# Branches B and C of a fused two-block kernel: two pieces of attention work in one step of TensorE, and the last tile summed from PSUM by VectorE

## The chip, the cores and the metric

One core of one Trainium2 chip runs the whole program. The metric is the device time of one execution in microseconds (us); lower is better. A measurement of one execution repeats within a few tenths of a per mille here (3111.25 to 3112.31 in three runs).

## The reference

Two blocks run one after the other on a sequence of 256 tokens of width 2048, in fp32. The first is one layer: a gated linear recurrence, and dilated attention in three groups of eight heads. The second, which the change touches, is a layer that is applied twice with other weights. Its core, shortened:

```python
def _hybrid_layer(x, ...):
    h = _rmsnorm(x, g_pre)
    ... = jnp.split(h @ w_in, SPLIT_POINTS, axis=-1)      # 2048 x 16192 weights
    o_a = latent attention, 8 heads of 128 (+ 64 rotated)
    # branch B: 8 heads, two softmax maps of width 64 each, values of 128
    a = softmax(q1 @ k1.T * s + mask) - lam * softmax(q2 @ k2.T * s + mask)
    o_b = _rmsnorm(a @ v, b_g_sub) * (1.0 - lam_init)
    # branch C: 8 heads of 128, one map, a bias by distance
    o_c = softmax(q @ k.T * s + bias) @ v
    y = sum over the three branches n of
        sigmoid(gate_n) * ((o_n * silu(z_n)) @ w_branch[n])
    return y @ w_out

for l in range(2):
    x = x + _hybrid_layer(x, l, ...)
```

With 256 tokens the attention is small: per head two score maps of 128 queries by 256 and 128 keys. Nearly all work is in the products with the weights, and every weight is used once.

## The kernel before

All activations are kept feature-major in SBUF (tiles of 128 features by 256 tokens). A weight product runs in **units**: a unit is 1024 rows by 256 columns of one weight matrix (1 MB), in two **halves** of 512 rows. SyncE loads a half into `raw` (line 383). ScalarE copies it into the high part of `hl` in a rounded 32-bit format (`hi`, line 952), and VectorE writes what that leaves out into the low part (`lo`, line 1310). TensorE then does, for each 128 rows and 128 columns, a wide matmul (high weights by high and low activations, 512 columns) and a narrow one (low weights by high activations, 256 columns); both are in `mm`, line 537. So a unit is 32 matmuls and a half 16. `hl` and `raw` hold two units: the split of unit n + 2 begins when TensorE has finished with the same half of unit n. Two units make a chunk of 256 output columns, whose two parts in PSUM (`pg`) are put together in SBUF: ScalarE copies the correction (`copy_corr`, line 960) and VectorE adds it (`join`, line 1317).

Attention is done by pairs of heads, four pairs per branch and layer, so branches B and C have eight pairs each in all. A pair has twelve units (0 to 11): queries, keys, values, a gate `z`, and four units of the branch's big gate. The small steps of the pair's attention stand between units, in PSUM `pa`, in full fp32. The order is written out by hand in the tables `EVENTS` (for TensorE), `ACT_EVENTS` (ScalarE, which for branch C is the same table) and `DVE_EVENTS` (VectorE). A word is a step with the numbers it runs over:

- `u9` is unit 9, `h20` half 20, that is the first half of unit 10 (`h21` its second, `h22` and `h23` those of unit 11)
- `s0`, `s1`: the scores of head 0 and 1 (TensorE, line 781); maxima (VectorE, lines 1584 and 1588) and exponentials (ScalarE, line 1133)
- `x0`, `x1`: VectorE turns the exponentials into probabilities (lines 1597 to 1605; line 1605 is the last operation of a head of branch B, and raises `probs_ready`)
- `t0`, `t1`: TensorE transposes the probabilities (line 788), after a wait for `probs_ready` and, for `t1` in branch B, for `pt_ready`; ScalarE copies the result to SBUF (line 1193) and raises `pt_ready`
- `p0`, `p1`: TensorE multiplies the values by them (lines 798 and 799); then, in branch C, VectorE's product with the gate (line 1719) and the split of the result by ScalarE (line 1139) and VectorE (`lo0`, `lo1`, line 1724); in branch B ScalarE's square (line 1196)
- `n0-1`: in branch B the norm of the result (line 889)

The engines run their tables side by side and meet at semaphores. Inside one engine the order of the table is the order of the instructions. A place at which TensorE's stream of line 537 is interrupted by such small steps is called a **break** below. The table `SIDE` names, by unit, the 128-row steps for which the wide matmuls of both columns come first and then both narrow ones: `FIRST` is the first step of a half or of the unit that begins there, `FIFTH` the fifth, where the second half begins.

The table's order around the change, before:

```python
"B": events("u0-4 norm u5-6 s0 u7-8 t0 s1 u9 p0 h20 t1 h21 p1 h22 n0-1 h23"),
"C": events("u0-4 norm u5-6 s0-1 u7-8 t0-1 u9 p0 u10 p1 u11"),
```

The last product of the program (`w_out` of layer two, added to `xres`) ends by bank: TensorE finishes the first 128 columns of the last chunk, raises `bank_done`, and then does the second (`last_unit_by_bank`, line 659). For each, ScalarE copies the correction (lines 967 and 969), VectorE joins it with the main part into `corr` (line 1325) and adds the sum to `xres` (lines 1875 and 1877), and SyncE stores it (lines 528 and 530).

Of the kernel before, what the change touches and what calls it, by code (L numbers as in the profile page):

```python
# [18 lines left out]
ALU = mybir.AluOpType  # L19
# [4 lines left out]
S = 256  # L24
D = 2048
NT = D // P
UC = 2048
CH = 256
NCH = D // CH
# [31 lines left out]
def events(text):  # L61

    out = []
    for word in text.split():
        what = word.rstrip("0123456789-")
        first, _, last = word[len(what):].partition("-")
        out += [(what, j) for j in range(int(first or 0), int(last or first or 0) + 1)]
    return out
# [3 lines left out]
EVENTS = {  # L72
    "1": events("u12-15 s0 u16-17 t0 u18 s1 u19-20 p0 t1 u21 p1 u22-23"),
    "A": events("u0-2 h6 rot norm h7-8 s h9-10 t0-1 h11 p0-1"),
    "B": events("u0-4 norm u5-6 s0 u7-8 t0 s1 u9 p0 h20 t1 h21 p1 h22 n0-1 h23"),
    "C": events("u0-4 norm u5-6 s0-1 u7-8 t0-1 u9 p0 u10 p1 u11"),
}


ACT_EVENTS = EVENTS | {  # L80
    "1": events("u0-11") + EVENTS["1"],
    "A": events("u0 q0 u1 q1 u2 h6 norm h7-8 s0-1 h9-10 t0-1 h11 p0-1"),
    "B": events("u0-4 norm u5-6 s0 u7-8 t0 s1 u9 p0 h20 t1 h21 p1 h22 n0-1 h23 o0-1"),
}
DVE_EVENTS = {
    "1": events("u0-2 rot0 u3-4 rot1 u5-6 rot2 u7-8 rot3 u9-10 rot4 u11-12 rot5 u13-15 s0 x0 u16-18 s1 x1 u19-20 p0 u21 lo0 p1 u22 lo1 u23"),
    "A": events("u0 q0 u1-2 h6 rot norm h7-8 s0-1 x0-1 h9-11 p0-1 lo0-1"),
    "B": events("u0-4 norm rot u5-6 s0 x0 u7-8 s1 x1 u9 h20-22 n0-1 h23 lo0-1"),
    "C": events("u0-4 norm u5-6 s0-1 x0-1 u7-9 p0 u10 lo0 p1 lo1 u11"),
}  # L90


# [2 lines left out]
FIRST, FIFTH, AGAIN = frozenset((0,)), frozenset((4,)), frozenset((RUNS, 4))  # L95
# [4 lines left out]
    "RG": {4: FIRST, 8: FIRST, 12: FIRST, 16: FIRST, 22: AGAIN, 24: AGAIN},  # L100
    "1": {16: FIRST, 18: FIRST, 19: FIRST, 21: FIRST, 22: FIRST},
    "A": {1: FIRST, 3: FIRST | FIFTH, 4: FIFTH, 5: FIFTH},
    "B": {5: FIRST, 7: FIRST, 9: FIRST, 10: FIRST | FIFTH, 11: FIRST | FIFTH},
    "C": {5: FIRST, 7: FIRST, 9: FIRST, 10: FIRST, 11: FIRST},
    "head": [{0: FIRST, 3: FIRST, 8: AGAIN, 12: FIRST, 14: FIRST}, {1: FIFTH, 2: AGAIN, 8: AGAIN, 12: FIRST, 14: FIRST}],
}

# [25 lines left out]
U_WO, C_WO = U_YA + 8, C_YA + 8  # L133
# [54 lines left out]
def build(nc, xT, w_in, w_gate, w_rnn, w_att, w_o, w_in2, w_uq, w_ukv, w_br, w_out2,  # L188
          vec1, vec2, blam, consts, tabs, bias_c, outT):
    ctx = ExitStack()  # L190
    with ctx:
# [35 lines left out]
        g3 = gat[:, :].rearrange("p (t n) -> p t n", n=S)  # L227
        cr = corr[:, :].rearrange("p (s t n) -> p s t n", s=2, n=S)
        pg3 = pg[:, :].rearrange("p (b n) -> p b n", n=512)
# [702 lines left out]
        def _(act):  # L932
            steps = Steps(act, act_steps)
# [26 lines left out]
                nc.scalar.activation(cr[:, cj % 2, 0:n, :], pg3[:, b:b + n, S:], ACT.Copy)\  # L960
                    .then_inc(corr_copied, 1 + skipped)

            def copy_corr_by_bank(u_last, c, n):

                act.wait_ge(bank_done, n + 1)
                act.wait_ge(evac_done, c + 1)
                nc.scalar.activation(cr[:, 1, 0, :], pg3[:, 2, S:], ACT.Copy).then_inc(bank_copied, 1)
                act.wait_ge(half_done, 2 * u_last + 2)
                nc.scalar.activation(cr[:, 1, 1, :], pg3[:, 3, S:], ACT.Copy).then_inc(corr_copied, 1)
# [242 lines left out]
            for c in range(NCH):  # L1212
                hi(U_WO + 2 * c, 2)
                if c < NCH - 1:
# [1 line left out]
                    hi(U_WO + 2 * c, 3)  # L1216
                    act.wait_ge(evac_done, C_WO + c + 3)
                    gained(m3, g3, post, tiles_of(c)).then_inc(y_scaled, 1)
            copy_corr_by_bank(U_WO + 2 * NCH - 1, C_WO + NCH - 1, 0)
            hi(U_L, 1, (0,))  # L1220
            norm_scale(1)
            act.wait_ge(evac_done, C_WO + NCH + 2)
# [11 lines left out]
            for l in range(2):  # L1234
                ul, cl_ = U_L + l * LU_N, C_L + l * LC_N
                for c in range(8):
                    for j in range(2):
                        if c == 2:
                            hi_rope_keys(ul + 6 + j, j, l)
                        else:  # L1240
                            hi(ul, 2 * c + j + 2)
                        if j == 0:
                            if c == 1 - l:
                                norm_scale(2 + l)
                            copy_corr(ul + 2 * c + 1, cl_ + c, c, 1 if c == 3 else 2)
                    if c == 2:
                        rope_keys_passed[0] += 1
                    if c in (1, 2):
                        split_h(1 + l, g3, (2 * c - 2, 2 * c - 1))
                    if c == 3:  # L1250
                        act.wait_ge(lam_prod, l + 1)
                        nc.scalar.activation(lam2, lam2, ACT.Exp).then_inc(lam_exp, 1)
                        act.wait_ge(evac_done, cl_ + 4 + 2)
                        nc.scalar.activation(m3[:, 6:12, :], m3[:, 0:6, :], ACT.Square)
                        nc.scalar.activation(m3[:, 12, :], kr, ACT.Square).then_inc(a_sq, 1)
                    if c == 5:
                        act.wait_ge(a_sum, l + 1)
                        rsqrt(nt3[:, 0, :], pa3[:, 0, 0:S], 1.0 / 512)
                        rsqrt(nt3[:, 1, :], pa3[:, 0, S:], 1.0 / 256)
                        rsqrt(nt3[:, 2, :], pa3[:, 1, 0:S], 1.0 / 64, a_rs)  # L1260
                        act.wait_ge(a_val, l + 1)
                        nc.scalar.activation(u3[:, 8:14, 0:S], m3[:, 6:12, :], ACT.Copy).then_inc(a_hi, 1)
                        nc.scalar.activation(u3[:, 15, 0:S], cst[:, P:3 * P], ACT.Copy).then_inc(ones_ready, 1)
                z_sigmoid(z3[:, 0:8, :], g3[:, 8:16, :], cl_ + LC["A"] + 2, PAIRS)
                for kind in "ABC":
                    turns = 2 if kind == "A" else 1
                    with act.Fori(0, PAIRS // turns) as i:
                        mark = steps.loop(i, ACT_PAIR_STEPS[kind] * turns)
                        for n in range(turns):
                            p = i * turns + n  # L1270
                            pair(kind, l, p, ul + LU[kind] + p * units(kind), cl_ + LC[kind] + p * CHUNKS[kind], 2 * n)
                    steps.end(mark, PAIRS // turns)
                    act.preload_act_table(ACT.Sigmoid)
                    half_product(ul + LU_BR[kind], cl_ + LC_BR[kind], G_L + l * G_N + NCH * PI[kind], kind == "C")
                    exp_table()
                uo, co = ul + LU_WO, cl_ + LC_WO
                if l == 0:
                    act.wait_ge(vec_landed, 48)
                for c in range(NCH):
                    if l == 0 or c < NCH - 1:  # L1280
                        hi(uo + 2 * c, 2)
                    if l == 1 and c == NCH - 1:
                        copy_corr_by_bank(uo + 2 * c + 1, co + c, 1)
                    else:
                        copy_corr(uo + 2 * c + 1, co + c, c)
                    if l == 0 or c < NCH - 1:
                        hi(uo + 2 * c, 3)
                    if l == 0:
                        act.wait_ge(evac_done, co + c + 3)
                        gained(u3, x3, v2[:, W_PRE:W_PRE + NT], tiles_of(c)).then_inc(hp_hi, 1)  # L1290
# [3 lines left out]
        def _(dve):  # L1294
# [21 lines left out]
                b = 2 * (cj % 2)  # L1316
                return tt(out, pg3[:, b:b + n, 0:S], cr[:, cj % 2, 0:n, :], ALU.add)  # L1317

            def join_bank(c, s, out, n=0):

                if s == 0:
                    dve.wait_ge(bank_copied, n + 1)
                else:
                    dve.wait_ge(corr_copied, c + 1)
                return tt(out, pg3[:, 2 + s, 0:S], cr[:, 1, s, :], ALU.add)
# [423 lines left out]
                    lo(U_WO + 2 * c, 3)  # L1749
            last = C_WO + NCH - 1  # L1750
            dve.wait_ge(n_sum, PRE_SUMS[0] + NCH)
            steps.done(join_bank(last, 0, g3[:, NT - 2, :], 0))
            tt(sq_new[:, 0, :], g3[:, NT - 2, :], g3[:, NT - 2, :], ALU.mult).then_inc(n_last, 1)
            join_bank(last, 1, g3[:, NT - 1, :]).then_inc(evac_done, 1)
            dve.wait_ge(evac_done, last + 3)
# [49 lines left out]
            for l in range(2):  # L1805
# [60 lines left out]
                for c in range(NCH):  # L1866
                    last = c == NCH - 1
                    if l == 0 or not last:
                        lo(uo + 2 * c, 2)
                    if l == 0 and c:  # L1870
                        gained_lo(pre, PAIR_TILES[c - 1], RAW_BASE[2] + c)
                    t, xt = cr[:, c % 2, :, :], x3[:, 2 * c:2 * c + 2, :]
                    if l == 1 and last:
                        steps.done(join_bank(co + c, 0, t[:, 0, :], 1))
                        tt(xt[:, 0, :], xt[:, 0, :], t[:, 0, :], ALU.add).then_inc(bank_stored, 1)
                        steps.done(join_bank(co + c, 1, t[:, 1, :]))
                        tt(xt[:, 1, :], xt[:, 1, :], t[:, 1, :], ALU.add).then_inc(evac_done, 1)
                        continue
                    steps.done(join(co + c, c, t))
                    tt(xt, xt, t, ALU.add).then_inc(evac_done, 1)  # L1880
                    if l == 0 and last:
                        lo(uo + 2 * c, 3)
                        gained_lo(pre, PAIR_TILES[c], RAW_BASE[2] + 1 + c)
                    if l == 0:
                        steps.done(chunk_squares(co + c, xt))
                        add_squares(PRE_SUMS[1] + 1 + c)
                    if not last:
                        lo(uo + 2 * c, 3)
# [96 lines left out]
```

## Time and profile before

| | |
|---|---|
| median of three runs | 3111.66 us (3111.25 to 3112.31) |
| the profiled execution | 3113.83 us, of which the span from first to last instruction is 3111.6 us |
| TensorE matmuls | busy 99% of the span, 18230 instructions |
| VectorE | busy 68%, 2741 instructions |
| ScalarE | busy 56%, 2290 instructions |
| DMA | 571.7 MB, mean 184 GB/s |
| mean granted TensorE clock | 0.998 of full |

A row of the timeline gives the start in us from the beginning of the span, the duration in us from the first to the last instruction of the row, the engine, the line of the kernel, the operation, what it writes and reads, its shape, and how many instructions the row stands for. Where the engine stood idle before it, that and the releaser follow in brackets. A full fp32 matmul of the small steps shows as two records. Ends of matmuls are modelled, so that consecutive rows overlap by a few tenths of a microsecond; starts are the better measure.

### The profile page before, as it was taken

Reading aid. Unit: us, or ns where it says so; the run is one execution under the profiler, and the core shown is the slowest. Engines: PE = TensorE matmul, PEld = TensorE weight load, DVE = VectorE, ACT = ScalarE, POOL = GpSimd, SP = SyncE. Lnnn points to the kernel's source line nnn. Section 1 sums busy time; section 2 is a strip of 40 time slices with the busy share of each in tenths; the row PEclk is TensorE's granted clock in tenths of the full one; section 3 lists DMA queues with packets and bytes.
Section 4 is the critical chain, followed back from the end, with each engine's and each line's share of the span. In section 5 each row is a group of like instructions: output and inputs, shape, how many; then the busy total and the mean of one; then the engine's idle time right before and its main releaser. Section 6 shows DMA issues by size and latency. Waiting matters only on the chain.

```text
span 3111.6 us, 52087 instructions
## 1 busy us (share of the span) xinstructions
PE 3090.1 (99%) x18230; PEld 2730.0 (88%) x18230; DVE 2128.2 (68%) x2741; ACT 1730.7 (56%) x2290; POOL 0.2 (0%) x4
## 2 busy tenths in 40 slices
PE   8999999999999999999999999999999999999999
PEld 7888888888888788888888888888888888888888
DVE  7677575766667687766766656777776676665675
ACT  5685444444445556656565555645665656555563
POOL 0000000000000000000000000000000000000000
PEclk9999999999999999999999999999999999999999
DMA  7656665555556655565556666566556555666555
GB/s 232 195 173 202 201 191 170 187 180 171 181 173 208 193 159 163 159 202 175 177 174 195 189 183 183 186 195 190 163 159 203 174 177 174 194 189 184 183 184 181
DMA packets 569813, 571.73 MB, mean 184 GB/s; under 512 B 26352, under 2 KB 565488, under 8 KB 569712
## 3 DMA queue, kind: packets, MB, share of 16 engines
q1 hardware_dynamic: 567440, 568.24, 59.2%
q10 hardware_dynamic: 2272, 2.18, 0.2%
q8 instruction: 60, 0.98, 0.1%
q14 instruction: 41, 0.34, 0.0%
HBM read 568.25 MB, written 2.10 MB: 183 GB/s over the span
## 4 chain that ended last, share of the span: by engine, by line
PE 95%; DVE 2%; ACT 1%; issue 1%; DMA 1%; SPq 0%; ACTq 0%; DVEq 0%
PE pg L537 89%; PE pa L781 1%; PE pa L798 1%; PE pa L788 1%; PE pa L537 1%; PE pa L754 1%; DVE hl L1310 1%; PE pa L799 1%; PE pa L711 0%; ACT hl L952 0%; DMA raw<-w_in 0%; PE pa L889 0%; DMA raw<-w_o 0%; SPq L472 0%; DVE mix L1848 0%
## 5 line engine op out<-in xcount | busy, mean ns | idle before, releaser
L537 PE MATMUL pg<-hT,hl 128*128 128x512 f32 x11456 | 1995.1, 334 | 0.4
L537 PEld LDWEIGHTS pg<-hT,hl 128*128 128x128 f32 x11456 | 1729.9, 188 | 227.6 <-DVE hl L1310 1.7
L1310 DVE TENSOR_TENSOR hl<-raw,hl 128x1024 fp32r<-128x1024 f32 (+1 forms) x1063 | 1249.8, 1213 | 293.1 <-ACT hl L952 285.5
L952 ACT ACTIVATE hl<-raw 128x1024 fp32r<-128x1024 f32 (+1 forms) x1063 | 1080.1, 1047 | 296.8 <-PE pg L537 275.3
L537 PE MATMUL pg<-uT,hl 128*128 128x256 f32 (+1 forms) x3712 | 630.5, 331 | 16.9 <-DVE hl L1515 7.9
L537 PEld LDWEIGHTS pg<-uT,hl 128*128 128x128 f32 x3712 | 555.1, 190 | 87.7 <-issue 15.9
L960 ACT ACTIVATE corr<-pg 128x512 f32<-128x512 f32 x286 | 170.3, 595 | 829.9 <-PE pg L537 829.9
L537 PE MATMUL pg<-hl,hT 128*128 128x512 f32 (+1 forms) x1792 | 318.5, 336 | 0.0
L537 PEld LDWEIGHTS pg<-hl,hT 128*128 128x128 f32 x1792 | 274.5, 188 | 38.6
L1317 DVE TENSOR_TENSOR work<-pg,corr 128x512 f32<-128x512 f32 (+1 forms) x154 | 105.8, 687 | 293.0 <-ACT corr L960 292.8
L1133 ACT ACTIVATE work<-work,sm 128x256 f32<-128x256 f32 (+3 forms) x144 | 69.3, 483 | 131.1 <-DVE sm L1588 129.2
L1317 DVE TENSOR_TENSOR gat<-pg,corr 128x512 f32 (+1 forms) x71 | 48.9, 689 | 132.8 <-ACT corr L960 132.8
L1317 DVE TENSOR_TENSOR xres<-pg,corr 128x512 f32<-128x512 f32 x32 | 22.1, 692 | 47.5 <-ACT corr L960 47.5
L1588 DVE TENSOR_REDUCE sm<-work 128x1 f32<-128x256 f32 (+3 forms) x144 | 49.0, 391 | 1.9
L1139 ACT ACTIVATE uT<-work 128x256 f32 x52 | 20.0, 414 | 53.2 <-DVE work L1719 53.2
L1597 DVE RECIPROCAL sm<-sm 128x2 f32<-128x2 f32 (+1 forms) x56 | 9.5, 170 | 50.3 <-ACT work L1133 50.3
L1584 DVE SCALAR_TENSOR_TENSOR work<-pa,tab 128x384 f32<-128x384 f32 (+2 forms) x56 | 43.6, 778 | 0.0
L798 PE MATMUL pa<-work 128*128 128x256 f32 x144 | 42.8, 378 | 0.0
L999 ACT ACTIVATE work<-pa,sm 128x256 f32<-128x256 f32 (+1 forms) x58 | 42.1, 725 | 1.2 <-PE pa L690 0.8
L995 ACT ACT_TABLE_LOAD x31 | 39.8, 1283 | 2.7 <-issue 2.2
L1317 DVE TENSOR_TENSOR corr<-pg,corr 128x512 f32<-128x512 f32 x15 | 10.4, 692 | 44.9 <-ACT corr L960 44.9
L1000 ACT ACTIVATE work<-work 128x256 f32<-128x256 f32 (+1 forms) x58 | 39.7, 685 | 1.9
(193 smaller groups left out, 1379.0 us busy)
## 6 DMA issues: line engine op xcount, KB each, us to landing
raw<-w_in SPq DMA_DIRECT2D x791, 512.0 KB, 4.6
raw<-w_br SPq DMA_DIRECT2D x96, 512.0 KB, 4.3
raw<-w_out SPq DMA_DIRECT2D x64, 512.0 KB, 4.7
raw<-w_rnn SPq DMA_DIRECT2D x32, 512.0 KB, 4.8
raw<-w_o SPq DMA_DIRECT2D x32, 512.0 KB, 5.2
raw<-w_att SPq DMA_DIRECT2D x16, 512.0 KB, 4.0
raw<-w_uq SPq DMA_DIRECT2D x16, 384.0 KB, 3.9
tab<-tabs SPq DMA_DIRECT2D x5, 896.0 KB, 6.5
```

Source lines behind the costliest of these rows:

```text
L537: return nc.tensor.matmul(out, lhsT, rhs, start=start, stop=stop, skip_group_check=True)
L798: nc.tensor.matmul(weighted(kind, e), va, pt[:, 0:S], start=m == 0, stop=False, skip_group_check=True)
L952: nc.scalar.activation(part(j, 0, h, 0, n), raw[:, bass.ds(j % 2 * UC + a, n)], ACT.Copy)\
L960: nc.scalar.activation(cr[:, cj % 2, 0:n, :], pg3[:, b:b + n, S:], ACT.Copy)\
L995: act.preload_act_table_set("natural_log_exp_and_others")
L999: steps.done(nc.scalar.activation(out, mean, ACT.Ln, bias=eps, scale=scale))
L1000: ins = nc.scalar.activation(out, out, ACT.Exp, scale=-0.5)
L1133: ins = nc.scalar.activation(part, part, ACT.Exp, bias=nmax[:, n:n + 1], accum_out=lsum[:, n:n + 1])
L1310: tt(part(j, 1, h, 0, n), raw[:, bass.ds(j % 2 * UC + a, n)], part(j, 0, h, 0, n).bitcast(F32), ALU.subtract).then_inc(lo_done, 1)
L1317: return tt(out, pg3[:, b:b + n, 0:S], cr[:, cj % 2, 0:n, :], ALU.add)
L1584: steps.done(stt(sc.rearrange("p (m n) -> p m n", m=nm), pa3[:, bank:bank + nm, 0:SM], SCALE[kind], tab[:, m0:m0 + SM * nm].rearrange("p ( ...
L1588: ins = nc.vector.tensor_reduce(nmax[:, n:n + 1], part, AX.XY if kind == "1" else AX.X, ALU.max, negate=True)
```

## The change

In the tables, branch B does the second transposes (`t1`) right behind the weighted values of head 0 (`p0`), ahead of half 20, on TensorE and ScalarE. Branch C does the weighted values of both heads behind unit 10, on all engines, and VectorE's splits behind both products. `SIDE` follows. For the last tile of the program ScalarE's copies go; VectorE adds the main part from PSUM to `xres` and then the correction from PSUM. The copy by bank with its counter argument remains at one other place, where it works as before.

```diff
-    "B": events("u0-4 norm u5-6 s0 u7-8 t0 s1 u9 p0 h20 t1 h21 p1 h22 n0-1 h23"),
-    "C": events("u0-4 norm u5-6 s0-1 u7-8 t0-1 u9 p0 u10 p1 u11"),
+    "B": events("u0-4 norm u5-6 s0 u7-8 t0 s1 u9 p0 t1 h20-21 p1 h22 n0-1 h23"),
+    "C": events("u0-4 norm u5-6 s0-1 u7-8 t0-1 u9-10 p0-1 u11"),
...
 ACT_EVENTS = EVENTS | {
-    "B": events("u0-4 norm u5-6 s0 u7-8 t0 s1 u9 p0 h20 t1 h21 p1 h22 n0-1 h23 o0-1"),
+    "B": events("u0-4 norm u5-6 s0 u7-8 t0 s1 u9 p0 t1 h20-21 p1 h22 n0-1 h23 o0-1"),
...
 DVE_EVENTS = {
-    "C": events("u0-4 norm u5-6 s0-1 x0-1 u7-9 p0 u10 lo0 p1 lo1 u11"),
+    "C": events("u0-4 norm u5-6 s0-1 x0-1 u7-10 p0-1 lo0-1 u11"),
...
 SIDE = {
-    "B": {5: FIRST, 7: FIRST, 9: FIRST, 10: FIRST | FIFTH, 11: FIRST | FIFTH},
-    "C": {5: FIRST, 7: FIRST, 9: FIRST, 10: FIRST, 11: FIRST},
+    "B": {5: FIRST, 7: FIRST, 9: FIRST, 10: FIRST, 11: FIRST | FIFTH},
+    "C": {5: FIRST, 7: FIRST, 9: FIRST, 11: FIRST},
...
-                    if l == 1 and c == NCH - 1:
-                        copy_corr_by_bank(uo + 2 * c + 1, co + c, 1)
-                    else:
-                        copy_corr(uo + 2 * c + 1, co + c, c)
-                    if l == 0 or c < NCH - 1:
+                        copy_corr(uo + 2 * c + 1, co + c, c)
                         hi(uo + 2 * c, 3)
...
                     if l == 1 and last:
-                        steps.done(join_bank(co + c, 0, t[:, 0, :], 1))
-                        tt(xt[:, 0, :], xt[:, 0, :], t[:, 0, :], ALU.add).then_inc(bank_stored, 1)
-                        steps.done(join_bank(co + c, 1, t[:, 1, :]))
-                        tt(xt[:, 1, :], xt[:, 1, :], t[:, 1, :], ALU.add).then_inc(evac_done, 1)
+                        for n, done in enumerate((bank_done, half_done)):
+                            dve.wait_ge(done, 2 * (uo + 2 * c + 1) + 2 if n else 2)
+                            steps.done(tt(xt[:, n, :], pg3[:, 2 + n, 0:S], xt[:, n, :], ALU.add))
+                            tt(xt[:, n, :], pg3[:, 2 + n, S:], xt[:, n, :], ALU.add)                                .then_inc(evac_done if n else bank_stored, 1)
                         continue
```

TensorE in a pair of branch B, before: around the second transposes (line 788). Lines 537 are the weight product; the names in brackets are the semaphores that the row waits for.

```order
L537 MATMUL pg<-hT,hl 128x512
L537 MATMUL pg<-hT,hl 128x256
L880 REGISTER_ALU
L788 MATMUL pa<-cst,work 128x128 [waits pt_ready,probs_ready]
L788 MATMUL pa<-cst,work 128x128 x2
L622 REGISTER_ALU
L537 MATMUL pg<-hT,hl 128x512 [waits lo_done]
```

And of the change, the same place of the pair:

```order
L798 MATMUL pa<-work 128x256 [waits pt_ready]
L799 MATMUL pa<-work 128x128
L880 REGISTER_ALU
L788 MATMUL pa<-cst,work 128x128 [waits pt_ready,probs_ready]
L788 MATMUL pa<-cst,work 128x128 x2
L622 ISA
L624 REGISTER_ALU [waits lo_done]
L537 MATMUL pg<-hT,hl 128x512 [waits evac_done]
```

The wait for `probs_ready` stood behind the sixteen matmuls of half 20. It now stands directly behind the weighted values of head 0 (lines 798 and 799), and half 20, which begins with the last row, behind it.

TensorE in a pair of branch C, the change, between units 10 and 11:

```order
L537 MATMUL pg<-hT,hl 128x256
L798 MATMUL pa<-work 128x256 [waits pt_ready]
L799 MATMUL pa<-work 128x128
L798 MATMUL pa<-work 128x256 [waits pt_ready]
L799 MATMUL pa<-work 128x128
L622 ISA
L537 MATMUL pg<-hT,hl 128x512 [waits lo_done]
```

Before, the first two of these four rows stood ahead of unit 10.

VectorE at the end of the program, before:

```order
L1310 TENSOR_TENSOR hl<-raw,hl 128x1024 [waits hi_done] x2
L1325 TENSOR_TENSOR corr<-pg,corr 128x256 [waits bank_copied]
L1875 TENSOR_TENSOR xres<-xres,corr 128x256 [waits dve_steps]
L1325 TENSOR_TENSOR corr<-pg,corr 128x256 [waits corr_copied]
L1877 TENSOR_TENSOR xres<-xres,corr 128x256 [waits dve_steps]
```

And of the change:

```order
L1307 TENSOR_TENSOR hl<-raw,hl 128x1024 [waits hi_done] x2
L1873 TENSOR_TENSOR xres<-pg,xres 128x256 [waits bank_done]
L1874 TENSOR_TENSOR xres<-pg,xres 128x256 [waits dve_steps]
L1873 TENSOR_TENSOR xres<-pg,xres 128x256 [waits half_done]
L1874 TENSOR_TENSOR xres<-pg,xres 128x256 [waits dve_steps]
```

The number of VectorE's operations is the same; each first one now waits for TensorE (`bank_done`, `half_done`) and no longer for ScalarE's copy. Lines behind line 963 have moved up by three in the changed kernel (1605 is 1602 there); those of TensorE are the same.

## Rows read from the trace of the kernel before

**Rows 1.** Page part 1 (busy us, share); all cores; TensorE's waits: us, times, longest.

```profile
PE 3090.1 (99%) x18230; PEld 2730.0 (88%) x18230; DVE 2128.2 (68%) x2741; ACT 1730.7 (56%) x2290; POOL 0.2 (0%) x4
...
core 0: 3111.6 us, clock 0.998
...
PE pg L537 <- DVE hl L1310: 1.4, 3, 0.7
```

**Rows 2.** Timeline, TensorE, pair of branch B, layer two: start us, us, engine, line.

```profile
2496.94 0.59 PE L798 MATMUL pa<-work 128*128 128x256 f32 x2
2497.37 0.38 PE L799 MATMUL pa<-work 128*128 128x128 f32 x2
2497.51 3.01 PE L537 MATMUL pg<-hT,hl 128*128 128x512 f32 x16
2500.35 0.49 PE L788 MATMUL pa<-cst,work 128*128 128x128 f32 x3
```

**Rows 3.** The same stretch, VectorE; [idle us before, and releaser].

```profile
2494.19 0.95 DVE L1584 SCALAR_TENSOR_TENSOR work<-pa,tab 128x768 f32<-128x768 f32 x1
2495.17 1.13 DVE L1588 TENSOR_REDUCE sm<-work 128x1 f32<-128x256 f32 x4
2498.23 0.18 DVE L1597 RECIPROCAL sm<-sm 128x4 f32<-128x4 f32 x1 [1.93 <-ACT work L1133]
...
2499.30 0.75 DVE L1605 SCALAR_TENSOR_TENSOR work<-work,sm 128x256 f32<-128x256 f32 x2
```

**Rows 4.** ScalarE in the same pair, from its third unit on.

```profile
2460.88 0.60 ACT L960 ACTIVATE corr<-pg 128x512 f32<-128x512 f32 x1 [4.46 <-PE pg L537]
...
2496.34 0.51 ACT L1133 ACTIVATE work<-work,sm 128x256 f32<-128x256 f32 x1 [3.13 <-DVE sm L1588]
```

**Rows 5.** Timeline, first pair of branch B, layer one: VectorE, TensorE.

```profile
1416.48 0.75 DVE L1605 SCALAR_TENSOR_TENSOR work<-work,sm 128x256 f32<-128x256 f32 x2
...
1417.53 0.49 PE L788 MATMUL pa<-cst,work 128*128 128x128 f32 x3
```

**Rows 6.** Chain of waits, longest undisturbed stretch: start us, us, engine, line, count.

```profile
1960.33 125.77 PE pg L537 x736
```

**Rows 7.** Timeline, TensorE, pair of branch C, layer two.

```profile
2754.84 0.59 PE L798 MATMUL pa<-work 128*128 128x256 f32 x2
2755.27 0.38 PE L799 MATMUL pa<-work 128*128 128x128 f32 x2
...
2760.97 0.59 PE L798 MATMUL pa<-work 128*128 128x256 f32 x2
```

**Rows 8.** The same pair after its unit 10: VectorE, ScalarE.

```profile
2764.98 0.43 DVE L1724 TENSOR_TENSOR uT<-work,uT 128x256 f32 x1 [0.82 <-ACT uT L1139]
...
2767.30 0.60 ACT L960 ACTIVATE corr<-pg 128x512 f32<-128x512 f32 x1 [2.59 <-PE pg L537]
```

**Rows 9.** Timeline at the hand-over after layer one's block: VectorE, TensorE.

```profile
1075.70 0.48 DVE L1391 SCALAR_TENSOR_TENSOR uT<-xres,v,uT 128x256 fp32r<-128x256 f32 x1 [0.39 <-ACT uT L1018]
...
1076.33 1.62 PE L537 MATMUL pg<-uT,hl 128*128 128x512 f32 x4 [3.33 <-DVE uT L1391]
...
1086.22 1.41 PE L537 MATMUL pg<-uT,hl 128*128 128x512 f32 x3 [3.84 <-DVE uT L1391]
```

**Rows 10.** Stretches: us, busy us per engine (instructions), PEclk, DMA share, GB/s.

```profile
1070.00:1100.00 30.00, 22.39 (x93) 18.12 (x92) 26.25 (x38) 19.00 (x32) 0.00 (x0) 0.77 0.55 161
...
1087.00:1092.00 5.00, 5.00 (x17) 4.23 (x17) 4.97 (x10) 3.83 (x7) 0.00 (x0) 0.50 0.00 0
1093.00:1098.00 5.00, 5.00 (x30) 4.34 (x30) 4.93 (x5) 0.48 (x2) 0.00 (x0) 1.00 0.82 256
```

**Rows 11.** Timeline, all engines, end of the program.

```profile
3108.21 0.38 ACT L969 ACTIVATE corr<-pg 128x256 f32<-128x256 f32 x1 [2.34 <-PE pg L537]
3108.63 0.42 DVE L1325 TENSOR_TENSOR corr<-pg,corr 128x256 f32<-128x256 f32 x1 [1.84 <-ACT corr L969]
3109.09 0.42 DVE L1877 TENSOR_TENSOR xres<-xres,corr 128x256 f32<-128x256 f32 x1
```

More of the change, by code:

```diff
@@ L961, in copy_corr, with copy_corr_by_bank @@
                     .then_inc(corr_copied, 1 + skipped)
-            def copy_corr_by_bank(u_last, c, n):
-                act.wait_ge(bank_done, n + 1)
+            def copy_corr_by_bank(u_last, c):
+                act.wait_ge(bank_done, 1)
                 act.wait_ge(evac_done, c + 1)
@@ L1218, in _ @@
                     gained(m3, g3, post, tiles_of(c)).then_inc(y_scaled, 1)
-            copy_corr_by_bank(U_WO + 2 * NCH - 1, C_WO + NCH - 1, 0)
+            copy_corr_by_bank(U_WO + 2 * NCH - 1, C_WO + NCH - 1)
             hi(U_L, 1, (0,))
@@ L1281, in _ @@
                         hi(uo + 2 * c, 2)
-                    if l == 1 and c == NCH - 1:
-                        copy_corr_by_bank(uo + 2 * c + 1, co + c, 1)
-                    else:
+                    if l == 0 or c < NCH - 1:
                         copy_corr(uo + 2 * c + 1, co + c, c)
-                    if l == 0 or c < NCH - 1:
                         hi(uo + 2 * c, 3)
@@ L1317, in join, with join_bank @@
                 return tt(out, pg3[:, b:b + n, 0:S], cr[:, cj % 2, 0:n, :], ALU.add)
-            def join_bank(c, s, out, n=0):
+            def join_bank(c, s, out):
                 if s == 0:
-                    dve.wait_ge(bank_copied, n + 1)
+                    dve.wait_ge(bank_copied, 1)
                 else:
@@ L1751, in _ @@
             dve.wait_ge(n_sum, PRE_SUMS[0] + NCH)
-            steps.done(join_bank(last, 0, g3[:, NT - 2, :], 0))
+            steps.done(join_bank(last, 0, g3[:, NT - 2, :]))
             tt(sq_new[:, 0, :], g3[:, NT - 2, :], g3[:, NT - 2, :], ALU.mult).then_inc(n_last, 1)
```

## The prediction

> **What bounds the kernel now.** I read the busy shares and the list of waits first. TensorE is busy 99% of the span, and outside the opening it waits for little: apart from two waits of 3.3 and 3.8 us where layer one hands over to the next block (at 1076 and 1086 us) no wait for VectorE's weight splits is over 0.7 us [rows 1, 9]. So the time is the length of TensorE's own stream. Whatever shortens the stream gains one for one, and every microsecond of a new wait in it is lost one for one.
>
> Then I read how fast the stream runs undisturbed. The chain of waits has a stretch of 736 matmuls of one kind in 125.77 us, 0.171 us each [rows 6]: 2.74 us for 16 (half a weight unit of 1024 rows by 256 columns) and 5.47 us for a unit of 32.
>
> Then the breaks. In branch C the weighted values of head 0 start at 2754.84 and those of head 1 at 2760.97 [rows 7]. Of these 6.13 us a unit of 32 takes 5.47, and the weighted values 0.64 (0.43 us from the first matmul of line 798 to the first of line 799, which has half as many columns and so 0.21). There remain 0.02 us for the break itself. In branch B it is 3.41 us from the weighted values of head 0 to the second transposes [rows 2], less 0.64 and less 2.74: 0.03 us. **A break costs almost nothing beside the work that it holds**; that is the most that moving two pieces together can save.
>
> Last, what the moved pieces wait for. The second transposes of a B pair (line 788) read the probabilities of head 1. VectorE writes these with the two operations of line 1605 that end at 2499.30 + 0.75 = 2500.05, and TensorE starts the transposes at 2500.35 [rows 2, 3]: 0.30 us to spare and no wait today. The same in the first B pair, with 1416.48 + 0.75 = 1417.23 against 1417.53 [rows 5]. The eight B pairs repeat this distance.
>
> **The change part by part.**
>
> *Branch B, second transposes moved ahead of half-unit 20.* They now stand right behind the weighted values of head 0, which end near 2497.51 + 0.07 = 2497.58 (2496.94 + 0.64) [rows 2]. The probabilities are still ready only at 2500.05. What brings them is a chain that the change leaves alone: VectorE takes the scores at 2494.19, ends the maxima at 2496.30, ScalarE begins the exponentials at 2496.34 and VectorE, which had waited 1.93 us for them, goes on at 2498.23 [rows 3, 4]. From VectorE's end to TensorE's restart I take 0.15 us, from the wait at 1076 us, where VectorE ended at 1075.70 + 0.48 = 1076.18 and TensorE began at 1076.33 [rows 9]. So the transposes start at 2500.20, 0.15 us sooner than now, after a **wait of 2.6 us**; and half-unit 20, whose 2.74 us covered that time so far, is done behind them. Net per pair: +2.74 - 0.15 = +2.59 us (the 0.03 us of the removed break is in it, since 2.74 is the undisturbed rate). Eight pairs: **+20.7 us**. Bounds: with no restart cost 8 x 2.44 = 19.5, with 0.15 more at each restart 21.9.
>
> Queued behind the waiting transposes are half-units 20 and 21, whose weights have long been split; behind them, on ScalarE and VectorE, the splits of the units after, which wait for TensorE's halves and so move along with it. ScalarE's copy of the transposes now stands ahead of a weight copy that waits for half-unit 20 anyway: nothing. The matmul order in half-unit 20 or 21 after a break (FIFTH left out): the same matmuls, nothing.
>
> The Trainium skill's page "TensorE: Matmul & The Clock Gate" speaks against this move (Part 2, step 1): only weight loads are pulled ahead in TensorE's queue, the matmuls stay in program order. By that, nothing of half-unit 20 can fill the wait; were they free to overtake, this term would be about zero. No row of the kernel before decides between the two.
>
> *Branch C, weighted values of head 0 moved behind unit 10.* One break fewer, 0.02 us, eight times: **-0.2 us**. The values have been waiting for longer, so no new wait. The products and splits of both heads now stand on VectorE and ScalarE behind unit 10. VectorE's last split of head 1 ends at 2764.98 + 0.43 = 2765.41 today; with head 0's two operations of 0.43 us there too it ends about 1 us later, by 2766.4. The next work of both starts at 2767.30, on TensorE's release [rows 8]. That cover is 0.9 us; if it were gone, weight splits would be later by some tenths, still several us ahead of their use.
>
> *The clock.* While busy, TensorE ran at the high level, and 30 matmuls started in 5 us; at the low level (1.2 GHz, shown as 0.50) 17 did [rows 10]. It was low around both waits of over 3 us: over 30 us there its mean is 0.77, which makes 0.23 x 30 / 0.5 = 13.8 us at the low level, 6.9 for each wait; over the whole span it is 0.998, so there was hardly any other [rows 1, 10]. The low level loses 1 - 17/30 = 0.43 us per us. A 2.6 us wait lies between 0.7 us, after which nothing fell, and 3.3 us, after which it did; it is nearer the second. Per wait the loss is between 0 and 6.9 x 0.43 = 3.0 us. I take 1.1: the wait is shorter, so I expect a fall at most of the eight, not all, and shorter ones. Eight: **+9 us**, between 0 and 24.
>
> *The last tile.* Behind the last matmul stand today ScalarE's copy (3108.21), VectorE's join (3108.63), VectorE's addition (3109.09) [rows 11] and then the store. The first goes, and VectorE waits for TensorE itself; two additions stay, which read PSUM and cost what line 1325 costs, 0.42. Gain 3108.63 - 3108.21: **-0.4 us**. The first half of the tile is 2.7 us sooner and is off the path.
>
> Sum: 20.7 - 0.2 - 0.4 + 9 = +29.1 us. The profiled execution took 3113.83 us, 2.2 over the median of the runs, 3111.66; it would take about 3143, and the median becomes **3140.8 us**, 0.9% more.
>
> **The rivals.**
>
> 1. *The wait comes, the clock holds.* Speaks for it: no wait of such a length is in the trace, and the nearest that changed the clock was longer. 3111.66 + 20.1 = 3131.8. The same page of the Trainium skill ("Why this matters for your kernels") warns only of longer pauses between bursts of matmuls; by its rule this rival is the result. The trace agrees for the waits over 3 us [rows 9, 10] and has none between. Chance 0.29.
>
> 2. *The clock falls for 6.9 us at all eight.* 3131.8 + 24 = 3156. Against: TensorE resumes sooner than in the two cases seen. Chance 0.05.
>
> 3. *The other side: the wait is paid once.* After the first wait TensorE is 2.6 us behind where it was against VectorE and ScalarE. If these carried that lead into the next pairs, the probabilities would be ready in time in the other seven: 2.6 us once, less 0.9 for breaks and tail: 3113.4, no change. The lead decides from 2.5 us on. Against: in each pair both engines come to stand before TensorE's halves, ScalarE for 4.46 us at 2460.88 [rows 4], 39 us before the probabilities, so the lead is gone before the next chain starts. Chance 0.05. If the probabilities came early in every pair by something not seen, 3110.8: chance 0.02, and it too is no change.
>
> **How the numbers follow.** Forecast (wait in every pair, clock low for part of the time, 3134 to 3150) 0.59; rivals 0.29, 0.05 and 0.07. For 8 times in 10 the range takes in the first rival with its lower bound (19.5 for 20.7, and a little) and stops short of the second: 3130 to 3153. A measurement here can tell about 0.2%, 6.2 us, from no change. Slower by more: 0.92; within: 0.07, rival 3; faster by more would need 6 us out of breaks worth 0.03 each: 0.01.
>
> **What would show it.** In the changed profile: eight waits of TensorE at line 788 for VectorE's line 1602 (today's 1605), 2.6 us each and 21 us in all; half-units 20 and 21 as one run of 32 matmuls; B pairs longer by 2.6 us, or more with a low clock; low stretches of the granted clock behind those waits; C pairs shorter by 0.02 us; between the last matmul and the last store two operations of VectorE, no copy of ScalarE. I am wrong if the waits are missing or shrink after the first pair, or if line 788 waits for ScalarE instead.

## The result and the profile after

| | before | changed |
|---|---|---|
| median | 3111.82 us (six runs, 3111.25 to 3112.31) | 3137.89 us (six runs, 3135.93 to 3139.76) |
| profiled execution | 3113.83 us, span 3111.6 | 3139.56 us, span 3137.4 |
| mean granted clock | 0.998 | 0.995 |

The changed kernel is slower by 26 us: the ratio is 1.0081, 95% interval 1.0070 to 1.0092. The forecast was 3140.8 us, range 3130 to 3153.

The page and the list of TensorE's waits (us in total, times, longest), changed kernel:

```profile
PE 3098.6 (99%) x18230; PEld 2737.0 (87%) x18230; DVE 2128.0 (68%) x2741; ACT 1731.8 (55%) x2288; POOL 0.2 (0%) x4
...
PE pa L788 <- DVE work L1602: 18.5, 8, 2.3
```

The wait shown is the one forecast; in the list of the kernel before line 788 does not stand, and [rows 2] show its transposes without a wait. There are eight waits, one for each pair of branch B. The share of busy time says nothing of it: TensorE still shows 99%. ScalarE has two instructions fewer (the last tile's copies).

TensorE in two consecutive pairs of branch B, layer two, changed kernel:

```profile
2440.12 0.90 PE L788 MATMUL pa<-cst,work 128*128 128x128 f32 x3 [2.33 <-DVE work L1602]
...
2451.05 1.02 PE L889 MATMUL pa<-work,cst 128*128 128x256 f32 x4
...
2512.75 0.59 PE L798 MATMUL pa<-work 128*128 128x256 f32 x2
2513.18 0.38 PE L799 MATMUL pa<-work 128*128 128x128 f32 x2
2515.85 0.55 PE L788 MATMUL pa<-cst,work 128*128 128x128 f32 x3 [2.28 <-DVE work L1602]
2516.15 5.70 PE L537 MATMUL pg<-hT,hl 128*128 128x512 f32 x32
...
2525.11 1.02 PE L889 MATMUL pa<-work,cst 128*128 128x256 f32 x4
...
2600.82 1.02 PE L889 MATMUL pa<-work,cst 128*128 128x256 f32 x4
```

And VectorE at the second of them:

```profile
2509.95 0.95 DVE L1581 SCALAR_TENSOR_TENSOR work<-pa,tab 128x768 f32<-128x768 f32 x1
2510.93 1.13 DVE L1585 TENSOR_REDUCE sm<-work 128x1 f32<-128x256 f32 x4
2513.99 0.18 DVE L1594 RECIPROCAL sm<-sm 128x4 f32<-128x4 f32 x1 [1.93 <-ACT work L1133]
...
2515.05 0.75 DVE L1602 SCALAR_TENSOR_TENSOR work<-work,sm 128x256 f32<-128x256 f32 x2
```

The chain is the one of [rows 3], with the same durations and the same 1.93 us for ScalarE's exponentials. It ends at 2515.05 + 0.75 = 2515.80, and the transposes start 0.05 us later. From the start of the last matmul ahead of the wait to the start of the first behind it are 2.6 us. Half-units 20 and 21 are one run of 32 matmuls, behind the wait: nothing of them was done in it.

The distance between two rows of line 889 is the length of a B pair. Before it is 71.60 us:

```profile
2435.25 1.02 PE L889 MATMUL pa<-work,cst 128*128 128x256 f32 x4
...
2506.85 1.02 PE L889 MATMUL pa<-work,cst 128*128 128x256 f32 x4
```

Here it is 74.06 for the pair that ends at 2525.11 and 75.71 for the one that ends at 2600.82. What sets the two lengths apart is the granted clock, which dropped behind the wait in the second of these pairs and not behind the one in the first; such a drop to the low level is called a fall below. Stretches of 10 us from the wait on (us, busy per engine, then the granted clock, DMA share, GB/s):

```profile
1414.00:1424.00 10.00, 7.70 (x47) 6.69 (x46) 6.08 (x11) 6.07 (x12) 0.00 (x0) 1.00 0.44 128
1488.00:1498.00 10.00, 7.66 (x37) 6.53 (x36) 5.79 (x10) 4.87 (x10) 0.00 (x0) 0.83 0.43 132
1564.00:1574.00 10.00, 7.72 (x38) 6.74 (x38) 5.79 (x10) 4.70 (x10) 0.00 (x0) 0.83 0.38 115
1639.00:1649.00 10.00, 7.68 (x46) 6.65 (x45) 5.80 (x10) 6.11 (x13) 0.00 (x0) 1.00 0.46 145
...
2438.00:2448.00 10.00, 7.88 (x37) 6.95 (x38) 5.79 (x10) 4.58 (x9) 0.00 (x0) 0.83 0.38 116
2513.00:2523.00 10.00, 7.72 (x47) 6.72 (x46) 5.81 (x11) 6.15 (x13) 0.00 (x0) 1.00 0.44 134
2588.00:2598.00 10.00, 8.05 (x40) 7.07 (x40) 5.79 (x10) 4.58 (x8) 0.00 (x0) 0.83 0.36 108
2663.00:2673.00 10.00, 7.65 (x39) 6.60 (x38) 5.79 (x10) 4.97 (x10) 0.00 (x0) 0.83 0.40 129
```

Behind five of the eight waits the mean over 10 us is 0.83, that is 0.17 x 10 / 0.5 = 3.4 us at the low level (1.2 GHz); behind three it is 1.00. With a fall 37 to 40 matmuls run in the stretch, without one 46 or 47.

The end of the program, changed kernel:

```profile
3134.38 0.42 DVE L1873 TENSOR_TENSOR xres<-pg,xres 128x256 f32<-128x256 f32 x1 [1.84 <-PE pg L537]
3134.84 0.42 DVE L1874 TENSOR_TENSOR xres<-pg,xres 128x256 f32<-128x256 f32 x1
3135.29 0.34 SPq L530 DMA_DIRECT2D out<-xres  x1
```

From TensorE's release to the store's issue it is 0.91 us. Before it was 1.33, from 3108.21 [rows 11] to the store's issue:

```profile
3109.54 0.34 SPq L530 DMA_DIRECT2D out<-xres  x1
```

### The profile page after: what moved, and what is told of

Read it like the earlier page. It is cut to its first block, busy times and chain, and to the rows that moved or that the text cites. A ratio compares the mean times of both kernels' runs of the same rounds, so it can differ in the third digit from the quotient of the medians.

```text
span 3137.4 us, 52084 instructions
## 1 busy us (share of the span) xinstructions
PE 3098.6 (99%) x18230; PEld 2737.0 (87%) x18230; DVE 2128.0 (68%) x2741; ACT 1731.8 (55%) x2288; POOL 0.2 (0%) x4
## 4 chain that ended last, share of the span: by engine, by line
PE 85%; DVE 5%; ACT 4%; issue 4%; DMA 1%; SPq 0%; ACTq 0%; DVEq 0%
PE pg L537 80%; ACT hl L952 2%; DVE hl L1307 1%; PE pa L798 1%; PE pa L781 1%; PE pa L788 1%; PE pa L754 1%; ACT work L1133 1%; DVE sm L1585 1%; PE pa L537 0%; PE pa L799 0%; DVE work L1581 0%; PE pa L711 0%; DMA raw<-w_in 0%; ACT work L999 0%
## 5 line engine op out<-in xcount | busy, mean ns | idle before, releaser
L788 PE MATMUL pa<-cst,work 128*128 128x128 f32 x216 | 31.7, 281 | 18.5 <-DVE work L1602 18.5
L788 PEld LDWEIGHTS pa<-cst,work 128*128 128x128 f32 x216 | 25.2, 143 | 21.1 <-DVE work L1602 20.0
```

The lines of the kernel that those rows point to most:

```text
L788: ins = nc.tensor.transpose(out[:, m, b * P:b * P + P], sc[:, SM * m + col:SM * m + col + P], ident)
```

## The experiments

The theory: all of the loss is TensorE's wait at line 788 in branch B, because the second transposes stand where VectorE has not yet written the probabilities, and the low clock behind some of these waits. The rivals: branch C's or the last tile's part also costs; joining two steps costs by itself; the wait is for something else than this chain. Branch B's part alone, branch C's with the last tile's, both steps behind half-unit 20, and the maxima ahead of the splits ran on one chip, where the kernel before took 3112.8 us (median of 27 runs, 3110.4 to 3115.7). The other four ran on another, where it took 3112.17 (16 runs, 3110.2 to 3114.1). So over more runs the kernel before spreads by up to 1.7 per mille, and not by the few tenths that three runs showed.

**Branch B's part alone.**

```diff
 before.py
-    "B": events("... u9 p0 h20 t1 h21 p1 h22 n0-1 h23"),
+    "B": events("... u9 p0 t1 h20-21 p1 h22 n0-1 h23"),
```

(the same in ScalarE's table, and `FIFTH` left out of unit 10)

> Only branch B's part of the change (second transposes right behind the weighted values of head 0). Theory (the loss is TensorE's wait for the probabilities of head 1 in each B pair, plus the low clock behind it): eight waits of 2.3 us at line 788, 18 to 19 us in all, clock low after four to eight of them; 3136 to 3141 us, that is all of the loss. Rival (the moved steps of branch C or the last tile also cost): the waits are the same but the time falls short of the whole change's 3137.9 by over 3 us.

Measured: 3138.3 us (3137.84 to 3139.28), ratio 1.0084 (1.0069 to 1.0100). TensorE's waits:

```profile
PE pa L788 <- DVE work L1605: 18.6, 8, 2.3
```

The whole loss is here, to within what runs differ by (25.5 us over the kernel before on the same chip, for 26.1). Four of the eight waits had a low stretch behind them.

**Branch C's and the last tile's part, without B's.**

```diff
 after.py
-    "B": events("... u9 p0 t1 h20-21 p1 h22 n0-1 h23"),
+    "B": events("... u9 p0 h20 t1 h21 p1 h22 n0-1 h23"),
```

(the same in ScalarE's table, and `FIFTH` back in unit 10)

> Branch C's part and the last tile's part, branch B as before. Theory: one break of 0.02 us fewer in eight pairs (-0.2 us) and ScalarE's copy of 0.4 us gone from the end: 3111.2 us, 0.6 under the kernel before. Rival (a break costs more than its gap in the stream shows, or the products of both heads behind unit 10 hold up the weight splits): 3109 or less, or 3113 and more with new waits of TensorE behind unit 11.

Measured: 3112.14 us (3110.83 to 3113.96), ratio 0.9998 (0.9989 to 1.0007): no difference that the time can tell. The stream can tell one. TensorE's scores in two consecutive C pairs, kernel before:

```profile
2736.46 1.47 PE L781 MATMUL pa<-work 128*128 128x128 f32 x8
...
2806.38 1.47 PE L781 MATMUL pa<-work 128*128 128x128 f32 x8
```

and here, with the joined step of a pair after them:

```profile
2734.20 1.47 PE L781 MATMUL pa<-work 128*128 128x128 f32 x8
...
2758.01 0.59 PE L798 MATMUL pa<-work 128*128 128x256 f32 x2
...
2758.66 0.60 PE L798 MATMUL pa<-work 128*128 128x256 f32 x2
...
2804.09 1.47 PE L781 MATMUL pa<-work 128*128 128x128 f32 x8
```

A C pair is 69.89 us and was 69.92: 0.03 us per break, and no wait came. VectorE's last split of head 1 ends 3.8 us after the weighted values of head 1 start (2761.67 + 0.77 - 2758.66), and ScalarE's next copy is at 2765.01, 2.6 us later:

```profile
2761.67 0.77 DVE L1721 TENSOR_TENSOR uT<-work,uT 128x256 f32 x2 [0.48 <-ACT uT L1139]
...
2765.01 0.60 ACT L960 ACTIVATE corr<-pg 128x512 f32<-128x512 f32 x1 [3.25 <-PE pg L537]
```

**The last tile's part alone.**

> Only the last tile's part: VectorE adds both parts from PSUM, no copy of ScalarE; branches B and C as before. Theory: 0.42 us between the last matmul and the end less, 3111.4 against 3111.8, which the time alone can hardly tell; in the profile 0.42 us less from the last matmul to the last store's issue. Rival (VectorE's additions from PSUM are slower than from SBUF, or start later behind TensorE's signal than ScalarE's copy did): the distance shrinks by under 0.2 us.

The edit: `after.py` with the tables and `SIDE` of `before.py`. Measured: 3112.12 us (3110.91 to 3113.37), ratio 0.9999 (0.9990 to 1.0008). From TensorE's release to the last store's issue:

```profile
3107.40 0.42 DVE L1873 TENSOR_TENSOR xres<-pg,xres 128x256 f32<-128x256 f32 x1 [1.84 <-PE pg L537]
...
3108.31 0.34 SPq L530 DMA_DIRECT2D out<-xres  x1
```

0.91 us for 1.33, so 0.42 less, as in the whole change. The time alone cannot show it.

**Both steps of branch B behind half-unit 20.** The same pieces joined, the other way round: the weighted values go back to the transposes, and not these ahead to them.

```diff
 after.py
-    "B": events("... u9 p0 t1 h20-21 p1 h22 n0-1 h23"),
+    "B": events("... u9 h20 p0 t1 h21 p1 h22 n0-1 h23"),
-    "B": {..., 10: FIRST, ...},
+    "B": {..., 10: FIFTH, ...},
```

(ScalarE's table as TensorE's)

> The whole change, but in branch B the weighted values of head 0 go back to meet the second transposes behind half-unit 20, where the probabilities are ready, and do not pull the transposes ahead of it. One break fewer as in the change. Theory (the loss is where the pair of steps stands, not that they are together): no wait at line 788, clock as before; 0.03 us less per B pair, with branch C and the tail 0.9 us in all: 3110.9 us. Rival (bringing the two steps together costs by itself, through the later weighted values or PSUM): over 3113 us.

Measured: 3110.99 us (3109.57 to 3112.40), ratio 0.9994 (0.9985 to 1.0004). No wait at line 788, and the clock is that of the kernel before, 0.998. TensorE in a B pair of layer two, and the end of the pair before it:

```profile
2432.41 1.02 PE L889 MATMUL pa<-work,cst 128*128 128x256 f32 x4
...
2496.82 0.59 PE L798 MATMUL pa<-work 128*128 128x256 f32 x2
...
2497.47 0.49 PE L788 MATMUL pa<-cst,work 128*128 128x128 f32 x3
2497.71 3.00 PE L537 MATMUL pg<-hT,hl 128*128 128x512 f32 x16
...
2503.97 1.02 PE L889 MATMUL pa<-work,cst 128*128 128x256 f32 x4
```

The pair is 71.56 us and was 71.60: joining the steps saves 0.04 us where nothing has to be waited for. So it is the place that costs, not the joining. This is the fastest of all kernels tried, but by 0.06% with an interval that holds no change.

**VectorE's maxima ahead of its weight splits.** TensorE's order is the change's; only VectorE's differs.

```diff
 after.py, DVE_EVENTS
-    "B": events("... s0 x0 u7-8 s1 x1 u9 ..."),
+    "B": events("... s0 x0 u7 s1 u8 x1 u9 ..."),
```

> The whole change, with one more edit on VectorE alone: in branch B the maxima of head 1 stand ahead of the two weight splits that follow unit 8. TensorE's order is that of the change. Theory (the wait is the length of the chain maxima, exponentials, probabilities behind the scores, in which VectorE's two splits of 1.2 us each come first): probabilities 2.4 us sooner, the wait at line 788 shrinks from 2.3 to 0 to 0.3 us, no clock falls, 3111 to 3113 us. Rival (the wait comes from ScalarE, or TensorE then waits for the split that was put behind): the wait at line 788 stays over 1 us, or waits of line 537 for the splits appear, 3120 us and more.

Measured: 3112.66 us (3111.91 to 3113.45), ratio 1.0000 (0.9991 to 1.0009). TensorE, then VectorE:

```profile
2497.00 0.38 PE L799 MATMUL pa<-work 128*128 128x128 f32 x2
2497.29 0.55 PE L788 MATMUL pa<-cst,work 128*128 128x128 f32 x3
```

```profile
2491.12 0.96 DVE L1581 SCALAR_TENSOR_TENSOR work<-pa,tab 128x768 f32<-128x768 f32 x1 [1.01 <-PE pa L781]
2492.11 1.13 DVE L1585 TENSOR_REDUCE sm<-work 128x1 f32<-128x256 f32 x4
2493.16 2.35 DVE L1307 TENSOR_TENSOR hl<-raw,hl 128x1024 fp32r<-128x1024 f32 x2
...
2496.49 0.75 DVE L1602 SCALAR_TENSOR_TENSOR work<-work,sm 128x256 f32<-128x256 f32 x2
```

VectorE now waits for the scores, and not they for it; the splits run while ScalarE takes the exponentials. The probabilities are there at 2497.24, and of the wait 0.08 us is left (2497.29, against 2497.00 + 0.21). All of the loss is gone with TensorE's order and `SIDE` untouched: the wait is this chain. Of the rival, TensorE's waits for weight splits (line 1307) did grow, from 1.4 to 2.9 us in all, but none of them is in a B pair; the longest, 1.2 us at 2108.53, stands between the layers, where the kernel before had one of 0.7.

**Maxima between the two splits.**

```diff
 after.py, DVE_EVENTS
-    "B": events("... s0 x0 u7-8 s1 x1 u9 ..."),
+    "B": events("... s0 x0 u7 h16 s1 h17 x1 u9 ..."),
```

> The whole change, with the maxima of head 1 on VectorE between the two weight splits that follow unit 8, so that one split and not two stands ahead of them. Theory: probabilities 1.2 us sooner than in the change, eight waits at line 788 of about 1.2 us; the stream is longer by 8 x 1.3 us less 0.9: 3121 us if the clock holds. On the clock: if a wait of 1.2 us is short enough that it never falls, no low stretch behind line 788 and 3121; if it falls as often as behind 2.5 us, up to 8 us more, 3129. Rival (the wait is not this chain): the wait stays 2.3 us, 3138.

Measured: 3121.94 us (3121.02 to 3126.32), ratio 1.0034 (1.0020 to 1.0047). TensorE's waits, one of them, and the clock of the stretch behind one:

```profile
PE pa L788 <- DVE work L1602: 9.5, 8, 1.2
```

```profile
2503.24 0.55 PE L788 MATMUL pa<-cst,work 128*128 128x128 f32 x3 [1.21 <-DVE work L1602]
```

```profile
1486.00:1496.00 10.00, 9.00 (x54) 8.01 (x55) 6.22 (x8) 4.83 (x7) 0.00 (x0) 1.00 0.66 196
```

The clock fell behind none of the eight, and a B pair is 72.97 us, 1.37 more than before. So in this execution the loss is the wait alone, and its length follows VectorE's order split by split. Of the five runs four took 3121.0 to 3122.0 us at a mean clock of 0.998, as the profiled one; the fifth took 3126.32 at 0.997. No trace of it was kept, so that a fall behind one of its waits is not excluded.

**Second transposes ahead of the weighted values too.**

```diff
 after.py
-    "B": events("... u9 p0 t1 h20-21 p1 h22 n0-1 h23"),
+    "B": events("... u9 t1 p0 h20-21 p1 h22 n0-1 h23"),
```

(the same in ScalarE's table)

> The whole change, but with the second transposes of branch B ahead of the weighted values of head 0 also. Theory: the transposes still start when the probabilities are there, the wait grows by the 0.64 us of the weighted values to about 3.1 us between matmuls, and these are done behind it: 8 x 0.64 = 5.1 us more, 3143. On the clock: if the fall depends on how long TensorE stands, more than five of the eight waits are followed by a low stretch, 1.5 us each, 3143 to 3147; if it is a matter of place alone, four or five as in the change, 3143. Rival (reordering in TensorE's queue, weighted values overtake the waiting transposes): as the change, 3138.

Measured: 3148.02 us (3145.91 to 3149.28), ratio 1.0115 (1.0099 to 1.0130), 9.2 us over the change on the same chip (below). TensorE, and two stretches of 10 us:

```profile
2594.82 0.90 PE L788 MATMUL pa<-cst,work 128*128 128x128 f32 x3 [2.99 <-DVE work L1602]
2595.51 1.06 PE L798 MATMUL pa<-work 128*128 128x256 f32 x2
```

```profile
2516.00:2526.00 10.00, 7.03 (x43) 6.04 (x42) 5.63 (x12) 6.06 (x14) 0.00 (x0) 1.00 0.49 152
2591.00:2601.00 10.00, 7.01 (x27) 5.86 (x26) 4.60 (x10) 5.00 (x13) 0.00 (x0) 0.66 0.50 156
```

The weighted values, whose operands are ready, do not overtake the waiting transposes. A pair without a fall is 74.76 us, 0.64 more than the 74.12 of one in the change: the 0.64 us of the weighted values, 5.1 for eight. If a longer wait made a fall more likely, I expected more than five; there were five, as the expectation had it for a matter of place, but two of them lasted twice as long (0.66 over 10 us is 6.8 us at the low level), and a pair with such a fall is 77.56 us, 2.8 more than without. Neither of the two expectations on the clock had that, and the time was 1 us over the upper end that I had given.

**The changed kernel again.**

> The changed kernel once more. Theory on the clock (which of the eight waits is followed by a low stretch depends on where the wait falls, not on the pair): again some but not all of the eight, and not the same pairs as in the first profile (second, third, fifth, seventh, eighth); a B pair 74.1 us long without and 75.7 with one. Rival (a fixed property of certain pairs): the same five.

Measured: 3138.83 us (3137.09 to 3139.21), ratio 1.0083 (1.0068 to 1.0099). The eight waits come to 18.6 us, for 18.5 in the first profile. The clock fell behind four of them, those of the second and fourth pair of layer one and the second and third of layer two; in the first profile it was the second and third, and the first, third and fourth. So it is no property of a pair. In the six runs of the result, three with a mean clock of 0.996 or 0.997 took 3135.9 to 3136.6 us and three with 0.995 took 3139.2 to 3139.8, which would fit one fall more or less at 1.6 us each. It is not shown that this makes the spread of 3.8 us: the kernel before spread over 5.3 us in 27 runs, all at a clock of 0.998, and the four runs of branch B's part alone do not follow their clock (3137.84 and 3137.98 us at 0.995, 3138.63 and 3139.28 at 0.996).

## Why the prediction was right

**What bounds the kernel.** As forecast: each microsecond of wait at line 788 came out as one of time. From a wait of 1.19 us to one of 2.33 and of 2.98 the pair without a fall goes from 72.97 us to 74.12 and 74.76, 1.15 and 0.64 more for 1.14 and 0.65. Waits of 0.1, 1.2, 2.3 and 3.0 us per pair gave 3112.7, 3121.9, 3138 and 3148 us in all, the last two with falls of the clock.

**The wait.** Forecast 2.59 us per pair net, measured 74.06 to 74.12 less 71.60, that is 2.5, or 20.0 us for the forecast 20.7. The size of the restart was wrong: TensorE starts 0.05 us behind VectorE's end and not 0.15. With 0.05 the sum of the prediction gives 2.74 - 0.25 = 2.49 us per pair, 19.9. Why it took 0.1 us longer at 1076 us was not tried.

**Order in TensorE's queue.** Half-unit 20 did not fill the wait of 2.3 us, and the weighted values did not fill the one of 3.0 in the last experiment but one. The Trainium skill's rule that matmuls stay in program order ("TensorE: Matmul & The Clock Gate", Part 2) holds here.

**The clock.** Forecast +9 us. A fall costs 75.71 - 74.06 = 1.6 us; five in the profiled execution make 8, four in two others 6.4. The mean of 1.1 us per wait came out at 0.8 to 1.0. The mechanism was right, and so was that not all of the waits would be followed by one, and that the stretches would be shorter (3.4 us for 6.9). That the size fits so well is in part luck: 1.1 was picked between 0 and 3.0, with no row on how often the clock would fall or for how long. Rival 1, the clock holds, fell: behind a wait of 2.3 us (2.6 us between the starts of two matmuls) the clock fell in 13 of 24 cases. The Trainium skill's page ("TensorE: Matmul & The Clock Gate", "Why this matters for your kernels") warns only of longer pauses; the measurement decides against that rule. Rival 2, a fall of 6.9 us at all eight, fell as well: there were five of 3.4.

**Rival 3, the wait is paid once.** It fell: the eight waits are all 2.3 us. ScalarE and VectorE do not carry their lead over from pair to pair. Elsewhere a wait did go: between the layers TensorE waited for a weight split before (the row below), and in the changed kernel it does not, nor in the two other profiles with waits of 2.3 us or the one with 3.0. All six profiles without such long waits have one wait more there than these, of 0.3 to 1.2 us. So the delay seems to help there; it was not tested.

```profile
2108.98 27.89 PE L537 MATMUL pg<-uT,hl 128*128 128x512 f32 x160 [0.68 <-DVE hl L1310]
```


**Breaks and the tail.** Forecast 0.03 us per break in B and 0.02 in C; the pairs became shorter by 0.04 and 0.03 where no wait was made. Tail: forecast 0.4, measured 0.42. VectorE and ScalarE in branch C had more cover than I gave them, 2.6 us and not 0.9, off the path in both cases. I had VectorE's last split 1 us later than before; counted from the start of head 1's weighted values it came sooner, 3.8 us behind it and not 4.4 (2765.41 - 2760.97 [rows 7, 8]).

**The sum.** 20.0 + 8 - 0.3 - 0.4 = 27.3 us against 25.7 between the two profiled executions. Of the rest 0.7 lies ahead of the first B pair, in code that the change does not touch (its weighted values start at 1413.44 and not at 1414.12); 0.6 is the wait between the layers that is gone (above); 0.3 I did not place.

## What to carry to other kernels

Before two steps are joined to save a change-over, measure the change-over (here 0.03 to 0.04 us of TensorE's time) and the slack of what the moved step reads (here 0.30 us, against 2.74 us of work that it was moved past). Where they are to be joined, move the step that is ready back, not the one that is not ready forward: the same join then cost nothing here. And where a producer is late, look at what stands ahead of it in its own engine's queue; here two splits of 1.2 us ahead of the maxima were the whole wait but 0.1 us.

## What the runs showed that was not expected

The clock fell behind waits well under 3 us, and not each time: behind none of eight of 1.2 us (one profile), behind five, four and four of eight of 2.3 us (three profiles), behind five of eight of 3.0 us, two of these for twice as long. A fall of 3.4 us cost 1.6 us of time. So in these profiles the pauses of 1.2 us cost their length, and those of 2.3 us and more cost more than that. What decides whether a given wait is followed by a fall was not tried.
